# An attention layer reordered: projections and their normalising units first, then one gate slab beside each head

## The reference, cut to what matters

```python
z = rms_norm(h, norm_g[l])
zp = jnp.einsum('btd,de->bte', z, w_in)
c_q, c_kv, k_pe, q_s, k_s, v_s, gate = split_cols(zp, EVEN_SPLITS)
y_a = mla_mixer(c_q, c_kv, k_pe, ...)      # 8 heads, full softmax; q and k rms-normed, 64 of 192 dims rotated
y_b = swa_mixer(q_s, k_s, v_s, ..., sink)  # 8 heads, band |q-k| <= 128 plus meta keys, one sink logit a head
y = jnp.concatenate([y_a, y_b], axis=-1) * jax.nn.silu(gate)   # gate: 2048 wide
return jnp.einsum('bte,ed->btd', y, w_out)
```

## Time and profile before

| what | value |
|---|---|
| median of 3 runs | 1698.6 us (1696.12 to 1698.62) |
| the profiled execution, its own time | 1694.27 us |
| its span, first to last instruction | 1692.5 us |
| PE, PEld, DVE, ACT busy | 94%, 91%, 67%, 53% of the span |
| mean granted TensorE clock | 0.983 |
| even layer's slabs and heads | about 20 to 347 us of the span |

### The profile page before, as it was taken

One profiled execution on the slowest core, in us unless ns is written; L12 is line 12 of the kernel. 1 busy time (PEld: TensorE's weight loads), 2 busy tenths in 40 slices (PEclk: granted clock), 3 DMA queues, 4 the chain that ended last, 5 costly groups with the idle time before them and its releaser, 6 DMA issues.

```text
span 1692.5 us, 32254 instructions
## 1 busy us (share of the span) xinstructions
PE 1594.2 (94%) x12490; PEld 1536.2 (91%) x12490; DVE 1141.7 (67%) x1734; ACT 902.7 (53%) x1416; POOL 48.4 (3%) x60
## 2 busy tenths in 40 slices
PE   7998797988889999999999999999999999999996
PEld 7988675987778999998999999999999899999996
DVE  4547668556877766667777766676666777786666
ACT  5464555457676444457554644454444766464443
POOL 0000000000000100000300000000000030000000
PEclk9999999989999999999999999999999999999998
DMA  5542300544444465545446555556555444555554
GB/s 195 165 150 87 97 1 1 163 149 149 130 141 153 130 198 185 185 160 164 161 126 207 168 186 185 186 165 208 184 186 185 140 157 140 188 163 188 185 185 136
DMA packets 73314, 263.66 MB, mean 156 GB/s; under 512 B 8144, under 2 KB 9680, under 8 KB 73104
## 3 DMA queue, kind: packets, MB, share of 16 engines
q1 hardware_dynamic: 70560, 252.66, 46.6%
q0 software_dynamic: 2672, 9.86, 1.8%
HBM read 261.43 MB, written 1.05 MB: 155 GB/s over the span
## 4 chain that ended last, share of the span: by engine, by line
PE 79%; DVE 11%; ACT 5%; issue 2%; DMA 2%; DVEq 0%; SPq 0%; ACTq 0%
PE PS L1453 23%; PE PS L1455 23%; PE PS L1454 23%; DVE w_lo L903 2%; PE PS L1686 2%; PE PS L1791 1%; DMA raw<-stream 1%; ACT w_hi L467 1%; DVE zf L1246 1%; PE PS L1630 1%; PE PS L1702 1%; PE PS L1464 1%; PE PS L1607 1%; DVE stat L1301 1%; ACT work L814 1%
## 5 line engine op out<-in xcount | busy, mean ns | idle before, releaser
L1453 PE MATMUL PS<-YH,w_hi 128*128 128x256 f32 (+1 forms) x2812 | 809.8, 288 | 19.8 <-DVE YL L1393 8.3
L1455 PE MATMUL PS<-YH,w_lo 128*128 128x256 f32 (+1 forms) x2812 | 796.5, 283 | 0.0
L1454 PE MATMUL PS<-YL,w_hi 128*128 128x256 f32 (+1 forms) x2812 | 796.4, 283 | 0.0
L903 DVE TENSOR_TENSOR w_lo<-raw,w_hi 128x1024 fp32r<-128x1024 f32 x476 | 584.0, 1231 | 213.5 <-ACT w_hi L467 210.0
L1453 PEld LDWEIGHTS PS<-YH,w_hi 128*128 128x128 f32 x2812 | 533.2, 190 | 27.5 <-issue 9.8
L467 ACT ACTIVATE w_hi<-raw 128x1024 fp32r<-128x1024 f32 x476 | 499.3, 1052 | 104.2 <-PE PS L1455 57.6
L1454 PEld LDWEIGHTS PS<-YL,w_hi 128*128 128x128 f32 x2812 | 533.0, 190 | 2.1 <-issue 0.5
L1455 PEld LDWEIGHTS PS<-YH,w_lo 128*128 128x128 f32 x2812 | 534.1, 190 | 0.0
L1453 PE MATMUL PS<-hH,w_hi 128*128 128x256 f32 x832 | 233.0, 280 | 6.4 <-DVE hL L996 6.4
L1454 PE MATMUL PS<-hL,w_hi 128*128 128x256 f32 x832 | 233.0, 280 | 0.0
L1455 PE MATMUL PS<-hH,w_lo 128*128 128x256 f32 x832 | 233.0, 280 | 0.0
(11 more groups left out here) (290 smaller groups left out, 1430.8 us busy)
## 6 DMA issues: line engine op xcount, KB each, us to landing
raw<-stream SPq DMA_DIRECT2D x476, 512.0 KB, 4.1
work<-stream POOLq DMA_DIRECT2D x16, 512.0 KB, 4.3
X<-x SPq DMA_DIRECT2D x1, 1088.0 KB, 5.0
out<-zf SPq DMA_DIRECT2D x8, 128.0 KB, 2.0
work<-rope SPq DMA_DIRECT2D x1, 544.0 KB, 8.0
work<-levels POOLq DMA_DIRECT2D x1, 512.0 KB, 4.0
work<-inv_count POOLq DMA_DIRECT2D x1, 512.0 KB, 4.8
work<-band POOLq DMA_DIRECT2D x1, 408.0 KB, 4.6
```

Of the source, the lines that this page charges most:

```text
L903: dve.tensor_tensor(w_lo[:, s.slot, :], raw[:, s.slot % RAW, :], f32(w_hi[:, s.slot, :]), ALU.subtract).then_inc(lo_ready, 1)
L1453: pe.matmul(to, wh, xh, start=start, stop=False, skip_group_check=True)
L1454: pe.matmul(to, wh, xl, start=False, stop=False, skip_group_check=True)
L1455: return pe.matmul(to, wl, xh, start=False, stop=stop, skip_group_check=True)
```

## The change

It touches the even layer only. (1) The projections now run windowed keys, windowed queries, MLA keys, MLA queries (rotated part first), MLA values, windowed values. (2) The 14 units stand between them, at slots `UNIT_AT`, in the order `pe`, `sk`, 4 `sq`, 4 `mk`, 4 `mq`; on DVE `finish(i-1)` now comes before `unit(i)`. The rotated key part's sum is added once, by DVE (`SQPE`), and no longer by TensorE in every `mk`. (3) The gate slabs leave this stage: gate slab n is multiplied beside head n, after `values(n-1)` and before the transposes of head n. The gate is Tanh on ACT and two products on DVE; Silu is gone, and the gate result is read from PSUM bank 7. `values` has one bank, 6. (4) For windowed heads TensorE adds the mask (identity by mask, float32r, into the scores' group); DVE reads the maximum from PSUM, and the sink is an Exp of 96x3 columns and one addition. (5) The latent planes of `YH`, `YL` are in use during the heads, so heads 0 to 7 go to slots 8 to 15 (`y_slot`), and the high and low parts of heads 8 to 15 are made beside the first 8 slabs of the output projection. The core of the diff, with the parts of ACT, of DVE and of PE in this order:

```diff
-        UNITS = [("pe", 0), ("sk", 0)] + [(kind, j) for j in range(4) for kind in ("mq", "mk", "sq")]
+        UNITS = [("pe", 0), ("sk", 0)] + [(kind, j) for kind in ("sq", "mk", "mq") for j in range(4)]
+        UNIT_AT = (7, 9, 11, 12, 14, 16, 17, 18, 19, 20, 21, 22, 23, 24)
...
+                act.wait_ge(job_out, {"pe": 6, "sk": J_QS, "sq": J_QS + 2 * j + 2, "mk": J_K + 2 * j + 2, "mq": J_Q + 2 * j + 6}[kind])
                 if i >= 2:
                     act.wait_ge(uss_done, i - 1)
-                    act.wait_ge(uout_ready, i - 3 if UNITS[i - 2][0] == "mk" else i - 1)
+                    if kind != "mk":
+                        act.wait_ge(uout_ready, i - 1)
...
+                def units_at(p):
+                    if p + 1 in UNIT_AT:
+                        unit_squares(UNIT_AT.index(p + 1))
+                    if p in UNIT_AT:
+                        unit_root(UNIT_AT.index(p))
...
-                for c in range(4):
-                    act.activation(G[:, 4 * c:4 * c + 4, :], G[:, 4 * c:4 * c + 4, :], ACT.Silu).then_inc(silu_ready, 1)
...
+                    if kind:
+                        act.activation(stat[0:96, b, 3, :], stat[0:96, b, 1, :], ACT.Exp,
+                                       bias=C[0:96, C_SINK + n - NH:C_SINK + n - NH + 1]).then_inc(sink_done, 1)
+                def gate(n):
+                    act.wait_ge(w_used, even(E_G + n).n + 1)
+                    act.activation(G[:, n, :], PS[:, 7, 0:T1], ACT.Tanh, scale=0.5).then_inc(ga_tanh, 1)
...
+                for n in range(2 * NH):
+                    split(even(E_G + n + LEAD))
+                    exps(n)
+                    if n == 3:
+                        act.wait_ge(m_loaded, 16)
+                        for t in range(3):
+                            act.activation(maskR[t], MASK[:, t, :], ACT.Copy)
+                        act.activation(identR, ident[:], ACT.Copy).then_inc(mr_ready, 1)
+                    gate(n)
+                    take_pt(n)
+                    if 2 <= n < NH + 2:
+                        high(n - 2)
...
+                def units_at(p):
+                    if p - 1 in UNIT_AT:
+                        finish(UNIT_AT.index(p - 1))
+                    if p in UNIT_AT:
+                        unit(UNIT_AT.index(p))
...
-                            step.step(dve.scalar_tensor_tensor(SB[b][0:m, t, 0:T1], src, qscale[0:m, n, t:t + 1], MASK[0:m, t, :],
-                                                               ALU.mult, ALU.add))
...
+                for n in range(2 * NH):
+                    shift(n)
+                    split(even(E_G + n + LEAD))
+                    if n:
+                        gated(n - 1)
+                    normalize(n)
+                    gate(n)
+                    if 3 <= n < NH + 3:
+                        low(n - 3)
+                gated(2 * NH - 1)
...
-                for i in range(16):
-                    from_z(even(E_G + i), job(J_G + i), None, T1)
-                    if i < len(UNITS):
-                        unit(i)
...
-                            last = pe.matmul(to, QS[:, h, m0:m0 + m], KS[:, h // 4, :], start=True, stop=True)
+                            pe.matmul(to, QS[:, h, m0:m0 + m], KS[:, h // 4, :], start=True, stop=False)
+                            last = pe.matmul(to, identR[:, 0:m], maskR[t], start=False, stop=True)
...
-                for n in range(2 * NH + 2):
-                    if n < 2 * NH:
-                        scores(n)
-                    if 1 <= n <= 2 * NH:
-                        turned(n - 1)
-                    if n >= 2:
-                        values(n - 2)
+                for n in range(2 * NH):
+                    scores(n)
+                    if n:
+                        values(n - 1)
+                        pe.wait_ge(gate_ready, n)
+                    from_z(even(E_G + n), PS[:, 7, 0:T1], None, T1)
+                    turned(n)
```

More of the change, by code:

```diff
@@ L1202, in c_scale @@
                                                  ALU.mult, ALU.mult).then_inc(cf_ready, 1)
[L1204 to L1215, removed]
                 def unit(i):
@@ L1575, in unit @@
                         for a in range(2):
-                            more = SQPE[:] if kind == "mk" else None
-                            last = pe.matmul(PS[:, a, 0:T1], ones[:], usq[b][:, a, :], start=True, stop=more is None)
-                            if more is not None:
-                                last = pe.matmul(PS[:, a, 0:T1], ones[:], more, start=False, stop=True)
+                            last = pe.matmul(PS[:, a, 0:T1], ones[:], usq[b][:, a, :], start=True, stop=True)
+                    else:
+                        pe.matmul(PS[:, 0, 0:T1], ones[:], SQPE[:], start=True, stop=True)
                     if kind in ("pe", "mq"):
@@ L1586, in unit, with units_at @@
                     last.then_inc(uss_done, 1)
-                pe.wait_ge(c_loaded, 16 * 3)
-                for i in range(16):
-                    from_z(even(E_G + i), job(J_G + i), None, T1)
-                    if i < len(UNITS):
-                        unit(i)
+                def units_at(p):
+                    if p in UNIT_AT:
+                        unit(UNIT_AT.index(p))
+                for i in range(2):
+                    from_z(even(E_KS + i), job(J_KS + i), None, T1)
+                    if i == 0:
+                        pe.wait_ge(c_loaded, 16 * 3)
+                        pe.wait_ge(cms_ready, 2)
+                    units_at(E_KS + i)
@@ new lines, in even_layer @@
+                for i in range(8):
+                    from_z(even(E_QS + i), job(J_QS + i), None, T1)
+                    units_at(E_QS + i)
+                pe.wait_ge(clo_ready, 5)
+                for i in range(2):
+                    s = even(E_K + i)
+                    pe.wait_ge(lo_ready, s.n + 1)
+                    for a in range(4):
+                        to = job(J_K + 4 * i + a)
+                        for k in range(2):
+                            last = mm3(to, s, 2 * a + k, cH[:, 3 + k, :], cL[:, 3 + k, :], k == 0, k == 1)
+                    last.then_inc(w_used, 1)
+                    units_at(E_K + i)
@@ new lines, in even_layer @@
+                for i in range(6):
+                    s = even(E_Q + i)
+                    pe.wait_ge(lo_ready, s.n + 1)
+                    for a in range(2):
+                        to = job(J_Q + 2 * i + a)
+                        for k in range(3):
+                            last = mm3(to, s, 3 * a + k, cH[:, k, :], cL[:, k, :], k == 0, k == 2)
+                    last.then_inc(w_used, 1)
+                    units_at(E_Q + i)
+                for i in range(2):
+                    s = even(E_V + i)
+                    pe.wait_ge(lo_ready, s.n + 1)
+                    for t, (m0, m) in enumerate(ROWS):
+                        to = job(J_V + 3 * i + t, m, 512)
+                        for k in range(2):
+                            last = rows3(to, (cH, cL), 3 + k, m0, m, s, k * 512, 512, k == 0, k == 1)
+                    last.then_inc(w_used, 1)
+                    units_at(E_V + i)
@@ L1596, in even_layer @@
+                for i in range(2):
+                    s = even(E_VS + i)
+                    pe.wait_ge(lo_ready, s.n + 1)
+                    for t, (m0, m) in enumerate(ROWS):
+                        to = job(J_VS + t, m, 256)
+                        for c in range(4):
+                            last = rows3(to, (zH, zL), 4 * i + c, m0, m, s, c * 256, 256, i == 0 and c == 0, i == 1 and c == 3)
+                    last.then_inc(w_used, 1)
                 pe.wait_ge(uout_ready, len(UNITS))
-                pe.wait_ge(job_out, J_ODD)
+                pe.wait_ge(job_out, J_END)
```

206 lines of the change are left out of this document (90 added, 116 removed).

## The result

| what | before | after |
|---|---|---|
| first comparison, median (4 runs each) | 1697.36 us | 1674.76 us (1672.35 to 1679.54) |
| second comparison, median (9 and 4 runs) | 1695.06 us | 1676.73 us (1674.58 to 1679.87) |
| profiled execution, its own time | 1694.27 us | 1675.49 us |
| its span | 1692.5 us | 1673.7 us |
| mean granted TensorE clock | 0.983 | 0.984 |

The ratio of the times is 0.9873 (95% interval 0.9846 to 0.9900) in the first comparison and 0.9896 (0.9881 to 0.9912) in the second, made later. The kernel is 1.0 to 1.3% faster. The spans differ by 18.8 us.

The account below looks back on a forecast made before the run. TensorE was taken to bound projections and MLA heads, VectorE windowed heads. First score 161.9, heads to 284.0, slab 0 at 288.8 instead of 302.0: 13.2 us off 1698.6 gives 1685.4 us, range 1678 to 1699.

Parts of the forecast that it names:

- Part 1: Projections with units, 42.8 to the first score: first score at 161.9 instead of 203.0, 41.1 us earlier.
- B: Projection units cost more in their new place, through more waits of some 1.5 us: 1691 us, chance 0.12.
- C: Low TensorE clock after the `mk` slots: up to 24.7 us more, 1710 us, chance 0.09.
- Part 2: Heads with gate slabs beside them: TensorE sets 8.15 us per MLA and 7.15 per windowed head, ending at 284.0.
- TensorE by head: Heads: sum of TensorE's work including gate slab 3.0 and entry 0.25, 8.15 us MLA and 7.15 windowed.
- entry of 0.25: Heads: extra TensorE time charged in each head when a gate slab's matmuls follow float32 work.
- The 1.0 for head 0: Heads: 1.0 us added because head 0 lacks the cover of `values`.
- Part 3: Into the output projection: slab 0 costs 4.8 us, done at 288.8 instead of 302.0.
- D: Better case: part 1's waits vanish (3.7), head 0 and clock cost nothing (2.5), shorter `mk` chain (1.5): 1678 us, chance 0.08.
- the waits of part 1: Projections: two TensorE waits, 2.1 us for ScalarE before `pe` and 1.6 for `finish(sk)` with its reciprocal.
- rival A: Heads: engine cycle binds, 8 us lost, 1693, chance 0.13; one form: each Exp costs a 1.28 us table load.

Follow-up runs that it names:

- Experiment 4: New kernel with the 128x544 reciprocal in the four `mk` units replaced by a product with 1 (keys wrongly scaled): 1659.98 us.
- experiment 2: New kernel with each gate slab cut in two halves around `values`, giving MLA heads one more change from float32 work: 1681.58 us.
- experiment 1: New kernel with 16 of the 24 matmuls of each gate slab left out: 1668.26 us.
- Experiment 7: New kernel with the gate slabs in a block ahead of the heads, heads in their old order: 1688.46 us, ratio to before 0.9960.

## Why the prediction was right in direction and short in size

**Part 1, right.** The reads of `mk` sums were predicted at 95.7 and 123.0 (end of the last), and measured at 95.64 and 122.56; the slot 8.9, measured 8.74; the finish of `mk3` 131.7, measured about 131.2; the first score 161.9, measured 161.9. The low clock was there as said (0.82 from 97 to 131, 0.78 to 137) and cost little: the chain, not TensorE, is the limit up to 131, and behind it twelve matmuls from 136.1 to 138.8 stood 0.23 apart instead of 0.125. That is some 1.2 us, where the prediction had put 1.5. Experiment 4 shows the chain to be the cause. Rivals B and C are out.

**Part 2, the failed step: "TensorE by head", its entry of 0.25.** The sum was 8.15 and 7.15; measured are 7.89 and 6.89, in every head behind head 0, and head 0 is shorter by its missing `values` alone, so 0.26 x 16 = 4.2 us. Without the entry term the prediction's terms add up to 7.89 and 6.89. The term came from the earlier trace rows: after float32 work the second matmul of a slab starts 0.33 behind the first, 0.2 more than usual. That gap is real, and it is there again (172.49 to 172.81): the slab takes 3.23 instead of 2.98. But one must look at the matmul before, too. By the starts of the matmuls the six passes of `values` in front of the slab take 1.19 us, where the kernel before has 1.43 for them (231.82 to 233.25). The 0.24 saved there pays for the 0.25 of the slab; scores (2.76 and 2.75) and transposes (0.71 and 0.72) are unchanged. The earlier trace rows showed it already: the float32 pair at 180.02 was followed after 0.34, not 0.46. In part 1 the 2.2 of an `mq` unit was read up to the slab's first matmul and had this in it, so the entry was rightly added there. In part 2 the 1.27 and 0.87 came from the weight loads of the earlier trace rows, where `values` were followed by float32 scores, and the gap from the matmuls of the earlier trace rows. Three further checks: a head without a slab is 4.89 and a slab 2.98 (30 us by 242 matmuls, times 24), sum 7.87; the mask in windowed heads is three more such entries, and the three scores with it take 1.76 (223.75 to 225.51) where the prediction had 1.38 + 0.37 = 1.75 with none charged; and a second entry in each MLA head changed TensorE's own period by 0.04 at most (experiment 2).

**The 1.0 for head 0** is the second term that failed, and it measured nothing. Head 0 has no `values` in front of its gate slab, but its transposes came at 167.78, 5.92 us after the first score at 161.86 and right behind the slab. The cycle of head 0 is 5.91 us (experiment 1), under the 6.3 to 6.8 of the prediction and just as long as its scores and slab: nothing to wait for. That the two are equal is luck; a longer cycle would have shown. Heads end at 278.8, predicted 284.0: 4.2 + 1.0 are the 5.2.

**Part 3** was 4.8 and took 4.6 (278.80 to 283.4). The slabs behind it are full as before, and DMA, one slab in 7 us, brought no wait. The prediction's 288.8 for slab 0 became 283.4, so the gain is 18.6 (302.0 - 283.4) instead of 13.2 us, and the spans say 18.8: what changed behind slab 0 is 0.2 us in sum.

**The median.** The forecast put 4.3 us between the profiled execution and the median, from three runs. With more runs the medians of before are 1697.36 and 1695.06, only 3.1 and 0.8 above it. Of the 10.6 us by which the forecast missed the median, 5.4 are the terms above, 0.2 are behind slab 0, and 5.0 are this (4.3 put on top, and a median that lies 0.7 under its own profiled execution).

**The range.** Its lower end, 1678, came from D, with the waits of part 1 gone. They did not go; two small costs in the heads did, one of them multiplied by sixteen. Still the traces alone stay inside it: 1698.6 less the 18.8 of the spans is 1679.8. The 5.0 us of the medians alone would have stayed inside as well. Both together went 3.2 us below. The range had no term for a median known from three runs, though single times of one kernel spread over 5 to 8 us.

**Table loads**: one for the whole stretch, so rival A's form is out, and the rule of the Trainium skill, "ScalarE: Activation LUTs", section on table sets, that exp and tanh share a set, holds in this order too. The granted clock was 1.00 in all of 161.9 to 278.8, float32 passes and transposes included. It was 0.82 where TensorE worked 20.06 of 34 us. Part 1 of "TensorE: Matmul & The Clock Gate" in the Trainium skill has the low clock as the default, which activity releases, and that row agrees. But the clock also fell to 0.50 from 137 to 139, where TensorE had been busy without a break since 132.8; why is open.

**What the prediction did not see** is why interleaving pays. It said that a slab beside an MLA head is not hidden, which is true (4.89 + 2.98 = 7.87), and then counted the gain of the heads as a whole without asking what a head costs without the slab once VectorE is lighter. Experiment 7 does. Nor did it say how much of the gain is the start of the stage, where Silu and the table loads of before had held back the first Exps (9.0 us by experiment 7's trace).

## What to carry to other kernels

A cost read as a gap between two starts belongs to a pair of instructions: take the period of the whole repeated stretch, with the work before and behind the seam and all of it from one timeline, before the gap is charged sixteen times. Here, interleaving two things that both kept one engine full (gate slabs and MLA heads) gained nothing in their middle; it hid the cycle of the windowed heads, and the fill, drain and low clock at the ends of the stage. These are what to add up. When one chain of small operations holds back a stage (here a root, two splits and a reciprocal of 3.54 us, four times), more work of the bound engine belongs into its slots, and moving units by a few places gave 7.5 us.

## What the runs showed of the hardware

A reciprocal of 128x544 float32 on VectorE takes 3.54 us, where a product of the same tile by a constant takes 0.44 and a read of it from PSUM 0.72. A scalar_tensor_tensor of 96x1 elements takes 0.216 us where it reads two further columns (L1323) and 0.155 where it reads one and has a constant (L1326); the two also differ in their second operation. By matmul starts, six float32 passes of 96x272 take 1.43 us in front of float32 scores and 1.19 in front of a slab, whose second matmul then starts 0.33 behind the first instead of 0.125. In experiment 7, TensorE was busy in all of 287 to 292 and was granted 1.2 GHz, after 1.8 us of waiting before the last transposes; in the new kernel the same float32 passes between slabs ran at 2.4 GHz throughout.
